# A hybrid decoder layer in fp32 parts: other places for gates, gelu of v, a weight split and VectorE's work in the first attention steps

## The reference, cut to what matters

```python
proj = h @ w_in
q, k_c, v_c, k_s, v_s, k_w, v_w, nsa_gl, u, v, merge_gl = split(proj)
nsa_gates = sigmoid(nsa_gl)                     # 24 a token
kc = silu(blocks(k_c + pe_ck) @ w_ck1) @ w_ck2  # 31 compressed blocks of 32 tokens
vc = silu(blocks(v_c + pe_cv) @ w_cv1) @ w_cv2
p_c = softmax(q @ kc.T);  o_cmp = p_c @ vc
o_sel = softmax(q @ k_s.T) @ v_s                # every causal block is among the 16 chosen
o_win = softmax(q @ k_w.T) @ v_w
o_nsa = gates[0]*o_cmp + gates[1]*o_sel + gates[2]*o_win
v = layer_norm(gelu(v));  mixed = tril(w_s) @ v + b_s      # in chunks of 128 tokens
o_sgu = gelu(u) * mixed
merged = sigmoid(merge_gl[0])*(o_nsa @ w_branch_nsa) + sigmoid(merge_gl[1])*(o_sgu @ w_branch_sgu)
h = layer_norm(ALPHA*h + merged @ w_out)
h = layer_norm(ALPHA*h + (silu(h @ w_gate) * (h @ w_up)) @ w_down)
```

## Time and profile before

| | |
|---|---|
| median of three runs | 765.35 us |
| the profiled execution | 765.74 us |
| its span | 764.0 us |
| PE busy | 739.3 us (97%) |
| DVE busy | 378.6 us (50%) |
| ACT busy | 306.3 us (40%) |
| POOL busy | 111.8 us (15%) |
| chain that ended last | 89% PE, 5% DVE, 3% issue |

### The profile page before, as it was taken

One profiled execution on the slowest core, in us unless ns is written; L12 is line 12 of the kernel. 1 busy time (PEld: TensorE's weight loads), 2 busy tenths in 40 slices (PEclk: granted clock), 3 DMA queues, 4 the chain that ended last, 5 costly groups with the idle time before them and its releaser, 6 DMA issues.

```text
span 764.0 us, 9665 instructions
## 1 busy us (share of the span) xinstructions
PE 739.3 (97%) x3709; PEld 623.3 (82%) x3709; DVE 378.6 (50%) x649; ACT 306.3 (40%) x467; POOL 111.8 (15%) x134
## 2 busy tenths in 40 slices
PE   7999997989999999999999999999999999999995
PEld 5889886868888897888789888888888888888884
DVE  2423267786778785675783232223322242233575
ACT  3522277456667676522344133323321232122511
POOL 2507070402334331000020000000000000000011
PEclk9999999999999999999999999999999999999998
DMA  9424214210111203634502322333233312332202
GB/s 262 146 86 153 68 56 149 72 55 1 56 56 56 56 1 104 227 110 163 169 24 73 125 91 73 110 110 105 63 106 110 110 59 107 111 110 71 94 28 82
DMA packets 57167, 72.73 MB, mean 95 GB/s; under 512 B 3856, under 2 KB 44336, under 8 KB 57136
## 3 DMA queue, kind: packets, MB, share of 16 engines
q1 hardware_dynamic: 57136, 72.32, 29.5%
HBM read 70.21 MB, written 2.10 MB: 95 GB/s over the span
## 4 chain that ended last, share of the span: by engine, by line
PE 89%; DVE 5%; issue 3%; ACT 2%; DMA 1%; POOL 0%; POOLq 0%; SPq 0%; ACTq 0%; DVEq 0%
PE ps L1253 79%; PE ps L1265 4%; PE ps L1261 3%; PE ps L1262 3%; DVE prob L1077 1%; DMA arena<-in_x 1%; DVE ptl L887 1%; DVE stat L1137 0%; POOL y L585 0%; ACT prob L779 0%; DVE atl L931 0%; DVE arena L1016 0%; DVE y L1162 0%; DVE wl L887 0%; DVE wl L877 0%
## 5 line engine op out<-in xcount | busy, mean ns | idle before, releaser
L877 DVE TENSOR_TENSOR wl<-stage,wh 128x2048 fp32r<-128x2048 f32 (+1 forms) x49 | 111.6, 2277 | 206.7 <-ACT wh L602 177.5
L1253 PE MATMUL ps<-wh,xh 128*128 128x512 f32 (+1 forms) x384 | 149.2, 388 | 0.0
L1253 PE MATMUL ps<-wh,xl 128*128 128x512 f32 (+1 forms) x384 | 147.4, 384 | 0.0
L1253 PE MATMUL ps<-wl,xh 128*128 128x512 f32 (+1 forms) x384 | 147.4, 384 | 0.0
L1253 PE MATMUL ps<-ath,wh 128*128 128x512 f32 (+1 forms) x384 | 146.2, 381 | 0.0
L1253 PE MATMUL ps<-atl,wh 128*128 128x512 f32 (+1 forms) x384 | 146.1, 380 | 0.0
L1253 PE MATMUL ps<-ath,wl 128*128 128x512 f32 (+1 forms) x384 | 146.1, 380 | 0.0
L602 ACT CAST wh<-stage 128x2048 fp32r<-128x2048 f32 x37 | 70.5, 1906 | 166.1 <-PE ps L1253 166.1
L1253 PEld LDWEIGHTS ps<-wh,xl 128*128 128x128 f32 x384 | 72.7, 189 | 14.1
L1253 PEld LDWEIGHTS ps<-wh,xh 128*128 128x128 f32 x384 | 72.7, 189 | 13.7 <-DVE wl L877 0.3
L1253 PEld LDWEIGHTS ps<-wl,xh 128*128 128x128 f32 x384 | 72.8, 190 | 13.5
(11 more groups left out here) (236 smaller groups left out, 1036.2 us busy)
## 6 DMA issues: line engine op xcount, KB each, us to landing
stage<-in_w_in SPq DMA_DIRECT2D x28, 512.0 KB, 4.5
stage<-in_w_ffn_gate SPq DMA_DIRECT2D x22, 512.0 KB, 4.6
stage<-in_w_ffn_up SPq DMA_DIRECT2D x22, 512.0 KB, 4.5
stage<-in_w_ffn_down SPq DMA_DIRECT2D x22, 512.0 KB, 3.9
stage<-in_w_out SPq DMA_DIRECT2D x8, 512.0 KB, 4.6
arena<-in_x SPq DMA_DIRECT2D x8, 256.0 KB, 5.5
stage<-in_w_in SPq DMA_DIRECT2D x8, 256.0 KB, 5.8
stage<-in_w_branch_nsa SPq DMA_DIRECT2D x4, 512.0 KB, 7.1
```

What stands on the lines that cost most here:

```text
L877: dve.tensor_tensor(wl[:, slot, 0:n], stage[slot][:, 0:n], wh[:, slot, 0:n].bitcast(fp32), ALU.subtract).then_inc(w_lo, 1)
L1253: return pe.matmul(out, (sh, sh, sl)[i], (mh, ml, mh)[i], start=start and i == 0, stop=stop and i == 2)
```

## The change

No arithmetic is added or removed. These instructions stand elsewhere:

- ACT computes the gates (`gates`, sigmoid) before the V projection's copies, and gelu of v right behind them. Before, both stood in the middle of the operand tiles.
- ACT and DVE split the compressed product's weight `U_CK` after operand tile 4; before, it came behind tile 7. The split of `U_MERGE0` stays behind the U projection's rows; tile 7 goes in between the rows.
- PE's `compress(0)` waits for `op_lo` 10 (the low parts up to tile 4); the waits for 12 and 16 stand behind it.
- DVE's low part of the second filling unit (`U_FILL0 + 1`) is made in three portions in steps 3, 4 and 5, and `weigh_cmp` in three parts at the ends of steps 0, 1 and 2.
- ACT's quarters of a merge unit come last in a step. `FILL_FIRST` is 2 for 3.

```diff
-    FILL_FIRST = 3
+    FILL_FIRST = 2
...
 # scalar (ACT)
             act.copy(pe_t[:, :, :], ps[:, 7, 0:32].rearrange("p (c j) -> p c j", c=2)).then_inc(pe_ok, 1)
+            act.wait_ge(raw_dve, 6)
+            act.wait_ge(raw_act, 6)
+            act.activation(gates[:, :, :, :, :].rearrange("p m g r b -> p m (g r b)"),
+                           kvb[:, :, 2 * P:2 * P + GATE_W], ACT.Sigmoid).then_inc(gates_ok, 1)
             chunk(U_V, 3, v_raw, SG, both=False)
+            act.wait_ge(raw_dve, 8)
+            act.wait_ge(raw_act, 8)
+            act.activation(v_raw, v_raw, ACT.Gelu_apprx_tanh).then_inc(gelu_ok, 1)
...
             split(U_U + 1, 1)
-            for t in range(2, 6):
+            for t in range(2, 5):
                 operand_hi(t)
-
-            act.activation(gates[...], kvb[...], ACT.Sigmoid).then_inc(gates_ok, 1)
-            act.wait_ge(raw_dve, 8)
-            act.wait_ge(raw_act, 8)
-            act.activation(v_raw, v_raw, ACT.Gelu_apprx_tanh).then_inc(gelu_ok, 1)
-            for t in range(6, 8):
-                operand_hi(t)
+            split(U_CK, 0)
+            operand_hi(5)
+            operand_hi(6)
             act.wait_ge(small_arrived, 160)
             hi(w2h[:, :, :], w2[:, :, :]).then_inc(w2_hi, 1)
-            chunk(U_U, 4, u_raw, SG)
+            take_rows(4, u_raw, SG, 0)
+            operand_hi(7)
+            take_rows(4, u_raw, SG, 2)
+            split(U_MERGE0, 1)
...
 # vector (DVE)
             split(U_U + 1, 1)
-            for t in range(2, 8):
+            for t in range(2, 5):
+                operand_lo(t)
+            split(U_CK, 0)
+            for t in range(5, 7):
                 operand_lo(t)
             dve.wait_ge(w2_hi, 1)
             lo(w2l[:, :, :], w2[:, :, :], w2h[:, :, :]).then_inc(w2_lo, 1)
-            chunk(U_U, 4, u_raw, SG)
+            dve.wait_ge(rows_done, 3 * 4 + 2)
+            dve.tensor_copy(u_raw[:, 1, :], ps[:, 1, :]).then_inc(raw_dve, 1)
+            operand_lo(7)
+            dve.wait_ge(w_used, U_U + 2)
+            dve.tensor_copy(u_raw[:, 3, :], ps[:, 3, :]).then_inc(raw_dve, 1)
+            split(U_MERGE0, 1)
...
             dve.tensor_tensor(rows, rows, per_row(cmax), ALU.subtract).then_inc(sc_max, 1)
-            fill_split(U_FILL0 + 1)
...
+            def first_fill(part):
+                u, cols = U_FILL0 + 1, slice(*((0, 512), (512, 1024), (1024, 2048))[part])
+                dve.wait_ge(w_hi, u + 1)
+                last = lo(wl[:, u % 2, cols], stage[0][:, cols], wh[:, u % 2, cols])
+                if part == 2:
+                    last.then_inc(w_lo, 1)
...
+                if 3 <= i < 6:
+                    first_fill(i - 3)
...
-                if i == 2:
-                    weigh_cmp()
...
+                if i < 3:
+                    weigh_cmp(i)
...
 # tensor (PE)
-            pe.wait_ge(op_lo, 16)
+            pe.wait_ge(op_lo, 10)
             compress(0, U_CK)
             pe.wait_ge(masks_ready, 3)
+            pe.wait_ge(op_lo, 12)
             for gs in range(4):
                 last = transpose(ps[:, 5, P * gs:P * gs + P], wsp[:, gs, :])
             last.then_inc(wt_done, 1)
             pe.wait_ge(raw_dve, 10)
             pe.wait_ge(raw_act, 10)
+            pe.wait_ge(op_lo, 16)
```

More of the change, by code:

```diff
@@ L613, in _, with take_rows @@
                     quarter_hi if k % 4 < 3 else w_hi, 1)
+            def take_rows(c, dst, n, m):
+                act.wait_ge(rows_done, 3 * c + m + 1)
+                act.copy(dst[:, m, :], ps[:, m, 0:n]).then_inc(raw_act, 1)
             def chunk(u, c, dst, n, n_next=2048, both=True):
@@ L618, in chunk @@
                 for m in (0, 2):
-                    act.wait_ge(rows_done, 3 * c + m + 1)
-                    act.copy(dst[:, m, :], ps[:, m, 0:n]).then_inc(raw_act, 1)
+                    take_rows(c, dst, n, m)
                 if both:
@@ L653, in _ @@
             split(U_U + 1, 1)
-            for t in range(2, 6):
+            for t in range(2, 5):
                 operand_hi(t)
-            act.activation(gates[:, :, :, :, :].rearrange("p m g r b -> p m (g r b)"),
-                           kvb[:, :, 2 * P:2 * P + GATE_W], ACT.Sigmoid).then_inc(gates_ok, 1)
-            act.wait_ge(raw_dve, 8)
-            act.wait_ge(raw_act, 8)
-            act.activation(v_raw, v_raw, ACT.Gelu_apprx_tanh).then_inc(gelu_ok, 1)
-            for t in range(6, 8):
-                operand_hi(t)
+            split(U_CK, 0)
+            operand_hi(5)
+            operand_hi(6)
             act.wait_ge(small_arrived, 160)
             hi(w2h[:, :, :], w2[:, :, :]).then_inc(w2_hi, 1)
-            chunk(U_U, 4, u_raw, SG)
+            take_rows(4, u_raw, SG, 0)
+            operand_hi(7)
+            take_rows(4, u_raw, SG, 2)
+            split(U_MERGE0, 1)
             act.wait_ge(raw_dve, 10)
@@ L764, in _ @@
                     take_o((i - 5) // 3)
[L766 to L772, removed]
                 if i in SOFT:
@@ L784, in _ @@
                     f_out += 1
+                for u, quarter in QUARTERS[i]:
+                    if quarter == 0:
+                        act.wait_ge(w_arrived[0], arrived(u)[1])
+                        act.wait_ge(w_used, u - 1)
+                    part = slice(512 * quarter, 512 * quarter + 512)
+                    last = act.copy(wh[:, u % 2, part], stage[0][:, part])
+                    last.then_inc(quarter_hi if quarter < 3 else w_hi, 1)
             for k in range(4):
@@ L1018, in _, with weigh_cmp @@
                                          op1=ALU.mult).then_inc(sgu_ok, 1)
[L1020 to L1031, removed]
+            def weigh_cmp(part):
+                if part == 0:
+                    dve.wait_ge(sc_exp, 1)
+                    step(dve.tensor_reduce(csum_f, rows, AX.X, ALU.add))
+                elif part == 1:
+                    step(dve.reciprocal(csum_f, csum_f))
+                    step(dve.tensor_tensor(csum, csum, any_block[:, :].rearrange(
+                        "p (g m k) -> p g m k", g=1, k=1).broadcast_to([P, G, MT, PAIRS]), ALU.mult))
+                    dve.wait_ge(gates_ok, 1)
+                    for g in range(G):
+                        step(dve.tensor_tensor(csum[:, g], csum[:, g], gates[:, :, g, :, 0], ALU.mult))
+                else:
+                    dve.tensor_tensor(rows, rows, per_row(csum_f), ALU.mult).then_inc(pcmp_ok, 1)
             def norm_prob(i):
```

## The result

The changed kernel takes 755.81 us (median of 5 runs, 755.22 to 756.30), the kernel before 765.35 us in the same session; the ratio is 0.9885 with a 95% interval of 0.9869 to 0.9901. By the medians the gain is 9.5 us, by the ratio 8.8 (7.6 to 10.0). Measured against the median before, the forecast of 757.5 us was a gain of 7.9 us; 755.81 is inside the range of 755.5 to 761.0, close to its lower end.

A forecast was written before the change was run, and what follows sets the result against it. PE, busy 97% of the span, bounds the kernel, so only its idle time and clock give time back. 765.74 - 4.4 (U projection) - 3.4 (attention) = 757.9, less 0.4 above the median: 757.5 us, range 755.5 to 761.0.

The forecast's parts named there:

- The gap is ACT's late split of the compressed weight: Between U projection and compressed product: PE's 3.97 us idle is a wait for that split, late on ACT behind gelu.
- the new wait: PE before the first merge unit, whose split must await U's end: 1.27 us, bounds 0 to 1.8 us.
- The half clock behind the gap goes, 1.7 us: Over 121 to 125, after the long wait, the mean clock was 0.57; full clock there would return 1.7 us.
- Gelu of v and gates hide in ACT's idle time: ACT before the tokens' copies: gelu ends 0.55 us before them, or makes them 0.73 us late; either costs nothing.
- DVE's chain behind the merge unit holds with 0.5 us to spare: DVE's v statistics through the hidden's low part end about 127.4, PE wants it about 127.8; overrun up to 0.5 us.
- The attention steps give 3.4 us: First attention steps: 1.8 us of idle time plus 1.7 us of half clock, 3.5, taken as 3.4 for handovers.
- So 1.8 us of idle time goes: First attention steps: PE waits fall from 2.46 us to 0.65 us; bounds 0 and 2.46.
- The pieces are 96 in all as before. I price both at 0: Attention's filling pieces, unchanged in number, and ACT's new order with exponentials first: neither counted as gain or loss.
- No wait over 0.5 us past step 3; the wait of 0.4 us in step 3: Sign in PE's attention profile: one 0.4 us wait in step 3, then scores without waits over 0.5 us.
- The 0.25 us in step 4: Second PE wait expected to remain in the first attention steps; with step 3's 0.4 us it makes 0.65.
- The third filling unit's load costs nothing: SP's load moves to about 172, lands 178, ACT wants it about 179: priced 0; slower case about 768, chance 0.03.
- The rival on the clock: Short waits still bring half clock at one of two places (759.2 us) or both (760.9 us); chance 0.17.

The follow-up runs named there:

- split_only: Kernel before with only the compressed weight's split (with tile 7 and PE's waits) moved, gates and gelu of v left between tiles 5 and 6; 761.90 us, ratio 0.9946.
- u_only: Kernel before with only the edits around the U projection (gates, gelu of v, compressed weight's split), attention steps as before; 760.18 us, ratio 0.9934.
- gelu_only: Kernel before with only gates and gelu of v moved, the compressed weight's split still behind tile 7; 762.36 us, ratio 0.9978.
- gelu_u_first: Changed kernel with gelu of u ahead of the first merge unit's split on ACT, lengthening PE's wait before that unit; 760.43 us, ratio 0.9944.
- att_only: Kernel before with only the attention edits (weigh_cmp and filling low part in portions, quarters last, FILL_FIRST 2); 760.39 us, ratio 0.9942.
- fill3: Changed kernel with FILL_FIRST 3 again; 757.73 us, ratio 0.9907.
- weigh_one: Changed kernel with weigh_cmp again in one piece in step 2; 757.76 us, ratio 0.9911.
- the halves: Changed kernel with the first merge unit's split made in two halves on ACT and DVE; 755.39 us, ratio 0.9878. With FILL_FIRST 1 added: 756.60 us, 0.9895.

## Why the prediction was right, and what was mis-sized

- *The gap is ACT's late split of the compressed weight.* Right, and shown by split_only: with the split moved and gelu left in place it is closed. The forecast put the new wait at 1.27 us and the gain at 4.37; they are 1.13 and 4.28 (u_only 4.30).
- *The half clock behind the gap goes, 1.7 us.* Right. That it belongs to the long wait is shown by the profiles of gelu_only (3.08 us, falls) and gelu_u_first (3.60 us, falls) against split_only (1.78 us, stays).
- *Gelu of v and gates hide in ACT's idle time.* Right to 0.04 us: 0.51 us of margin where 0.55 was worked out. DVE's copy of the compressed weight took 2.60 us beside POOL, 2.82 assumed.
- *DVE's chain behind the merge unit holds with 0.5 us to spare.* Right so far as PE shows no wait there.
- *The attention steps give 3.4 us.* The mechanism is right, the size is not: 5.6 us (att_only 5.57). This is the term that failed, in two steps.
  - "So 1.8 us of idle time goes" counts the idle column of the list, and a wait costs more than that. The last filling matmul before the wait of 1.45 us starts at 169.27 and the score at 171.12; in the change the last filling matmul starts at 161.79 and the score at 162.02. That is 1.85 us for 0.23, and until the score's second matmul it is 0.10 us more. So the waits of 0.65 and 1.45 us cost 0.92 and 1.72 us, 2.64 together. (The U part was worked out from starts, and came out to 0.1 us.) The one of 0.36 us is still there as 0.33.
  - "The pieces are 96 in all as before. I price both at 0": the table of FILL_FIRST 2 is worth 1.4 us by fill3, 0.8 of it from step 15 on. Step 18 alone, whose wait of 0.38 us at 203.69 the kernel before had and the prediction doesn't name, gives 0.62 us.
  - With the clock's 1.7, as said, that is 5.0 of the 5.6 us. The last 0.6 us are stops of 0.1 to 0.3 us in later steps, too short for the list, some gone and some new; no run takes them apart.

The filling matmul before the wait of 1.45 us, before the change:

```profile
169.27 0.40 PE L1253 MATMUL ps<-xh,wl 128*128 128x512 f32 x1
```

The same place in the change, with the score behind it:

```profile
161.79 0.39 PE L1280 MATMUL ps<-xh,wl 128*128 128x512 f32 x1
162.02 0.22 PE L1288 MATMUL ps<-ath 128*128 128x128 f32 x1
```

- *No wait over 0.5 us past step 3; the wait of 0.4 us in step 3.* Right: one of 0.33. The 0.25 us in step 4 didn't come.
- *The third filling unit's load costs nothing.* Right: ACT's first quarter started at 172.07 with no wait before it.
- *The rival on the clock*, by which many short waits bring it down. In the change's profile it didn't come true. weigh_one is the harder case: 1.46 and 0.49 us within 2 us, PE busy 2.06 of 4 us, and 1.00 behind it, while 0.65, 0.36 and 1.48 us over 8 us brought the clock down in the profile of u_only, as in those of before, gelu_only and split_only. The Trainium skill (TensorE: Matmul & The Clock Gate, "A second HAM failure mode: psum-queue depth-cycling") lets frequent short idles bring the clock down. The profiles with three such waits agree, weigh_one's with two of them does not, and what tells the two cases apart stays open. It need not be the waits: not every execution of one kernel has the fall (last section), and each case is read from one profile a kernel.

## What to carry to other kernels

Where a wait is put down to "issue", look on the engines that feed the waiting one for an instruction that ends 0.1 us before it, and then for what stands ahead of *that*: here a weight split stood behind work nobody was waiting for. Price a PE gap by the starts of the matmuls on its two sides, and with the half clock behind it: in the profiles here a lone one of 3.1 us or more cost 1.6 to 1.7 us on top, one of 1.8 us nothing. And where filling work is spread by rounding over many steps, compare in each step what it covers with the chain that it has to cover (here 2.03 us over ACT and DVE), and treat the table as a parameter to be measured; its value was 1.4 us for one piece and its sign isn't monotone (3, 2 and 1 pieces ahead: +1.42, 0 and, on the halves, +1.31 us).

## What was not expected of the hardware

- The half clock at the start of the program lasts differently from one profile to another: to 11.7 us in the profile before, to 8.7 us in the one after, with the same work and about the same arrival of data. It is worth 1.4 us of span here, and with effects of 1 us it must be taken out before two spans are compared.
- ACT's table load ran ahead of the wait of the activation it serves (87.20, while V's rows came at 89.94), so a switch of function in front of a wait cost nothing.
- Each fall of the clock cost the same, 1.71 us summed from the windows, in the profiles of before (twice), u_only, att_only, gelu_only (twice), split_only and gelu_u_first.
- A fall isn't in every execution of a kernel. One minus the mean granted clock, times the span, is the time missing at half clock. The profile of before has 3.4 us of it from its two falls and 2.3 us from the end of the program, where PE has nothing to do (0.54 over 759 to 764); the profiles of all the kernels have 2.2 to 3.6 us there. But 14 of the 40 executions of before in the three later sessions have a mean clock of 0.995, 3.8 us missing, which leaves no room for both falls; these are its shortest, 762.7 to 763.7 us. Four of gelu_only's 12 executions and two of split_only's 7 have 0.997, 2.3 us missing, which leaves room for none. They were not profiled, so which fall was absent, and why, is not shown. How much a change wins by the clock therefore depends on how often the kernel before had fallen, which is one more reason to read single effects from the stretch.
